# Zero products of TensorE in the pauses of a single-core, two-block network kernel

## What is computed

```python
def first_block(x, ...):                      # two layers
    # layer 0: recurrent block (projections, conv, gates, scan), layer 1: attention
    for layer in range(2):
        mix = rg_lru_block(x, ...) if layer == 0 else stick_breaking_attention(...) @ attn_w_out
        x = layer_norm(DN_ALPHA * x + mix, ln_g[layer, 0], ln_b[layer, 0])
        f = conv_ffn(x, ...)                  # 1024 -> 2 x 3072 -> 1024
        x = layer_norm(DN_ALPHA * x + f, ln_g[layer, 1], ln_b[layer, 1])

def second_block(x, c, ctx, ...):             # two layers, with 256 context tokens beside x
    for layer in range(2):
        h = rmsnorm(x, g) * (1 + sc1) + sh1   # shifts and gains from silu(c) @ mod_w
        x = x + g1 * mixer(h)                 # layer 0: Fourier and convolution; layer 1: softmax attentions
        h2 = rmsnorm(x, g) * (1 + sc2) + sh2
        x = x + g2 * hier_moe(h2)             # 32 experts of 1024 -> 512 -> 1024, 2 per token
    return rmsnorm(x, final_norm_g)
```

## Time and profile before

| | us |
|---|---|
| median of 3 runs | 2388.82 |
| lowest and highest | 2386.5, 2391.74 |
| the profiled execution | 2387.36 |
| its span, first to last instruction | 2385.3 |
| PE busy | 2134.5 (89%) |
| PE weight loads busy | 1330.0 (56%) |
| DVE busy | 849.8 (36%) |
| ACT busy | 368.4 (15%) |
| mean granted clock of PE | 0.953 |

### The profile page before, as it was taken

One profiled execution on the slowest core, in us unless ns is written; L12 is line 12 of the kernel. 1 busy time (PEld: TensorE's weight loads), 2 busy tenths in 40 slices (PEclk: granted clock), 3 DMA queues, 4 the chain that ended last, 5 costly groups with the idle time before them and its releaser, 6 DMA issues. The chain is left out here.

```text
span 2385.3 us, 27394 instructions
## 1 busy us (share of the span) xinstructions
PE 2134.5 (89%) x10410; PEld 1330.0 (56%) x10410; DVE 849.8 (36%) x1774; ACT 368.4 (15%) x695; POOL 23.6 (1%) x26
## 2 busy tenths in 40 slices
PE   7999998979999979979999999967989898888884
PEld 6788887657888844545444444425546433333332
DVE  3466664044666659441111111113263311111112
ACT  2411112042111130220000000002222100000001
POOL 0000000000000000000000000010000000000000
PEclk9999999999999989989999999988989899999997
DMA  7546556412566671306999999975221499999994
GB/s 272 212 177 247 211 211 246 162 50 90 213 247 241 215 298 42 135 36 278 427 428 426 427 426 426 426 311 213 74 103 71 186 426 427 427 428 427 426 427 186
DMA packets 138469, 638.09 MB, mean 268 GB/s; under 512 B 7120, under 2 KB 10224, under 8 KB 104496
## 3 DMA queue, kind: packets, MB, share of 16 engines
q1 hardware_dynamic: 120928, 595.48, 62.5%
q0 software_dynamic: 5600, 21.27, 2.5%
q10 hardware_dynamic: 11888, 20.62, 2.3%
HBM read 606.41 MB, written 30.93 MB: 267 GB/s over the span
## 5 line engine op out<-in xcount | busy, mean ns | idle before, releaser
L688 PE MATMUL T<-ring,S 128*64 128x512 f32 x2112 | 502.7, 632 | 71.7 <-DMA ring<-in_exp_w_up 68.5
L688 PEld LDWEIGHTS T<-ring,S 128*64 128x64 f32 x2112 | 157.3, 144 | 370.7 <-issue 365.0
L576 PE MATMUL T<-X,ring 128*128 128x256 f32 x1536 | 339.3, 380 | 2.4 <-ACT X L1036 2.4
L576 PEld LDWEIGHTS T<-X,ring 128*128 128x128 f32 x1536 | 292.1, 191 | 42.2 <-issue 2.6
L711 PE MATMUL T<-ring,S 128*64 128x512 f32 x1056 | 238.0, 592 | 1.2 <-DVE S L1529 1.2
L1325 DVE SCALAR_TENSOR_TENSOR S<-ring,cs,S 128x512 f32<-128x512 f32 x336 | 229.4, 744 | 0.0
L1523 DVE TENSOR_TENSOR S<-S,T 128x256 f32<-128x256 f32 x66 | 27.8, 421 | 498.0 <-ACT S L1104 498.0
L676 PE MATMUL T<-S 128*128 128x128 f32 x1600 | 188.2, 279 | 14.2 <-DVE S L1404 14.2
L676 PEld LDWEIGHTS T<-S 128*128 128x128 f32 x1600 | 185.2, 195 | 14.4 <-issue 7.9
L584 PE MATMUL T<-S,ring 128*128 128x256 f32 x768 | 176.7, 383 | 16.1 <-DVE S L1355 16.1
L584 PEld LDWEIGHTS T<-S,ring 128*128 128x128 f32 x768 | 143.4, 190 | 51.7 <-DVE S L1355 33.4
(11 more groups left out here) (265 smaller groups left out, 1452.0 us busy)
## 6 DMA issues: line engine op xcount, KB each, us to landing
ring<-in_exp_w_gate SPq DMA_DIRECT2D x66, 2048.0 KB, 16.6
ring<-in_exp_w_up SPq DMA_DIRECT2D x66, 2048.0 KB, 21.1
ring<-in_exp_w_down SPq DMA_DIRECT2D x66, 2048.0 KB, 23.4
ring<-in_ffn_w_up SPq DMA_DIRECT2D x24, 2048.0 KB, 12.7
ring<-in_mod_w SPq DMA_DIRECT2D x24, 2048.0 KB, 7.9
ring<-in_ffn_w_down SPq DMA_DIRECT2D x12, 2048.0 KB, 7.8
y_rows<-S ACTq DMA_DIRECT2D x132, 128.0 KB, 7.6
y_rows<-zb POOLq DMA_DIRECT2D x4, 3072.0 KB, 23.5
```

The lines of the kernel that those rows point to most:

```text
L576: ins = pe.matmul(T[:, m % 2, h * S:(h + 1) * S], w[:, k, m * P:(m + 1) * P], x1[:, k, :], start=(k == 0), stop=(k == KT - 1))
L688: ins = pe.matmul(T[c * B:(c + 1) * B, s, :].rearrange("p (g n) -> p g n", g=2), xgT[:, k, s * B:(s + 1) * B], ring[:, 3 * s:3 * s + 2, k ...
```

## The change

A helper `keep_busy(n, bank_)` issues n products of the zero tile with itself, 128 x 512 in bfloat16, into bank 5 or bank 1. They carry no semaphore and wait for none. Eleven calls are added.

```diff
+            def keep_busy(n, bank_=5):
+
+                for _ in range(n):
+                    pe.matmul(T[:, bank_, :], zb[:, 0:P], zb[:, :], start=True, stop=True)
+
             def layer_norm(i):
...
                 ins.then_inc(ln_mean, 1)
+                keep_busy(5)
...
                     if i == 0:
                         ins.then_inc(g_used, 2)
+                else:
+                    keep_busy(6)
                 pe.wait_ge(ln_rs, i + 1)
                 spread(S, LN_STD).then_inc(ln_bc, 1)
+                keep_busy(4, 1)
...
             def norm(r, k_tiles=KT, n=N2, sq=S1, off=0):
                 norm_sums(r, k_tiles, n, sq, off)
+                keep_busy(6)
                 norm_spread(r, n)
+                keep_busy(6)
...
                         ins.then_inc(full[u % 4], 1)
+                keep_busy(8)
                 pe.wait_ge(r["m_ready"], l + 1)
...
+                keep_busy(24 - 8 * l)
                 turn_tokens(t0)
                 up(t0, 0)
...
                 down(tl, 1)
+                keep_busy(80 - 20 * l, 1)
...
                 dense(c0["q"] + j, 4, lambda k: x1[:, k, :], u0["q"] + 2 * j, S)
+            keep_busy(12)
             read(pe, u0["q"] + 3)
             read(pe, u0["v"] + 3)
...
             pe.wait_ge(s_late, 16 * N_LATE)
+            keep_busy(20)
             norm(0)
...
                           start=True, stop=True).then_inc(full[(u + j) % 4], 1)
+            keep_busy(28)
             pe.wait_ge(cd_rot, 2)
```

## The result

| | before | changed |
|---|---|---|
| median, us | 2389.4 | 2371.27 |
| runs, lowest to highest, us | 6, 2386.15 to 2391.74 | 6, 2366.71 to 2376.81 |
| profiled execution, us | 2387.36 | 2370.43 |
| its span, us | 2385.3 | 2368.6 |
| mean granted clock of PE | 0.953 | 0.978 |

The ratio is 0.9928, with a 95% interval of 0.9916 to 0.994: 0.7% faster, 18.1 us. The forecast was 2370.3.

The account below looks back on a forecast made before the run. Outside the transfer-bound expert loops, PE spent 159.8 us at half clock, worth 39.3 us at most. The terms summed to -18.5 us: 2387.4 - 18.5 + 1.5 = 2370.3 us as a median, range 2362 to 2384.

Parts of the forecast that it names:

- the likeliest case: Whole kernel: the forecast itself, 18.5 us saved, median 2370.3 us, chance 0.68.
- Layer norms 0, 1, 3, norms 0, 2, 4: Work behind these norms returns to full clock: -1.6, -2.4, -4.2 (layer norm 3 with norm 0), -2.6, -2.1 us.
- Attention: 12 products ahead of the first scores, where only 0.69 us pause, delay ScalarE's read of them: +1.8 us.
- I count no clock gain: Attention: the long 3.52 us pause behind the scores stays empty, so no clock gain, at best 0.7 us.
- Layer norm 2: Has no low stretch in the earlier profile, so its products gain 0.
- Norm 3: 6.36 us of work at half clock, 3.2 at most; its sums keep empty gaps: -2.0 us.
- Route 0: 24 products leave 2.5 us empty and the clock may fall again; two thirds of 2.8 at most: -2.0 us.
- Route 1: Half of 6.29 us of work is 3.1; 16 products leave 2.9 us idle: -2.0 us.
- Last layer's attentions: 28 products fill 6.2 of 8.19 us; gain 2.5 at most, half taken because 2.0 us stay idle: -1.3 us.
- products at half clock and too many: Rival: zero products cost 0.44 us each and overrun the pauses, 49 us slower, 2437 us; chance 0.06.
- half of it given back: Rival: remaining idle and light work let the clock fall again; only 6 us gained, 2382.8 us; chance 0.18.
- the transposes: Rival: transposes hold the clock down for the 8 products behind them in each route; +1.4, 2371.7 us; chance 0.02.

Follow-up runs that it names:

- e1: The changed kernel with every zero product cut from 512 to 8 columns; 2391.69 us, ratio 1.0004 to the kernel before.
- e2: The changed kernel with zero products only in the layer norms, the norms and the 20 in front of norm 0; 2372.47 us, ratio 0.9932.
- e4: The changed kernel with the attention's 12 products removed and 14 put behind the first two heads' scores, in the pause before the suffix sums; 2367.07 us.
- e5: e4 with more products in the routes, behind the expert phases and before the last attentions, and 2 for 6 behind norms 2 and 4's spreads; 2366.76 us.
- e11: e4 without norm 3's 12 products and the 80 behind expert phase 0; 2368.79 us, ratio 0.992 to the kernel before.
- e3: The changed kernel with zero products only in the routes, before the attentions and before and behind the expert phases, none in layer norms and norms; 2387.94 us.
- e8: The changed kernel without the six and six zero products in norm 3; 2371.0 us, ratio 0.9918 to the kernel before.
- e6: The changed kernel without the 80 and 60 products behind the expert phases; 2372.54 us, ratio 0.9921 to the kernel before.
- e9: The changed kernel unchanged, profiled in a second execution; 2368.38 us.
- e7: The changed kernel with 24 instead of 12 products in front of the attention's first scores; 2370.77 us, ratio 0.9918 to the kernel before.

## Why the prediction was right, and where not

The changed kernel came out at 2371.27 for 2370.3: the likeliest case held, and it is right for its stated reason, by e1 (the clock) and e2 (the norms). That it is right to 1 us is partly luck: single terms were off by 2, with both signs, and the runs lie over 10 us.

Two readings in it were loose, and nothing hangs on them. A 9 in the earlier trace rows is 0.9 or more, so that row cannot tell 1.0 from 0.9. And the rank products' 5.6 us are not among PE's longest waits: its list of waits has, among others outside the loops, 16.1 us in the FFNs (18 waits), 13.0 in front of the suffix sums, 9.7 in front of the norms' sums and 8.2 in front of the last layer's scores. Of the terms:

- **Layer norms 0, 1, 3, norms 0, 2, 4.** Forecast 1.6 + 2.4 + 4.2 + 2.6 + 2.1 = 12.9, measured 1.55 + 2.33 + 4.26 + 2.62 + 1.90 = 12.66. The spreads are at 1.10 us. What worked was to take half of PE's work at half clock from the earlier trace rows, where the products behind have their operands. The prediction had only bounds for a zero product at half clock. The Trainium skill ("TensorE: Matmul & The Clock Gate", "Wait — 56ns, not 53.3ns?") has 427 ns for such a product at the low clock; the trace agrees. In the low stretch from 1617.2 three products stand between 1617.62 and the spread at 1618.90, 0.43 us each; six at full clock take 1.46 in all, 0.22 apart. Timeline of the changed kernel, norm 3:

```profile
1617.62 1.49 PE L544 MATMUL T<-zb 128*128 128x512 bf16 x3
1618.90 1.86 PE L537 MATMUL T<-std,tab 128*128 128x128 f32 x8
1620.60 1.46 PE L544 MATMUL T<-zb 128*128 128x512 bf16 x6
```

- **Attention: the step that was mis-sized, +1.8, measured +4.03.** The placement cost 1.55, as ScalarE's timeline shows: 3.46 us from its last read of the q products to the scores' in the changed kernel, 1.91 in e4 (two fences, in this order).

```profile
480.79 0.60 ACT L1093 ACTIVATE S<-T 128x512 f32<-128x512 f32 x1 [6.31 <-PE T L521]
...
484.25 0.60 ACT L1093 ACTIVATE S<-T 128x512 f32<-128x512 f32 x1 [1.55 <-PE T L820]
```

```profile
480.15 0.60 ACT L1094 ACTIVATE S<-T 128x512 f32<-128x512 f32 x1 [6.31 <-PE T L521]
...
482.06 0.60 ACT L1094 ACTIVATE S<-T 128x512 f32<-128x512 f32 x1
```

  That is near the 1.8 forecast. The other 2.5 us are the clock, and the step "I count no clock gain" left out that it could also be lost. The clock fell already in front of the first suffix sums, which before made at full clock (1.05 us more over the heads), and again at 528.3 in the output projection, 29.33 us where before took 27.89 in its first execution (1.44). The projection's part isn't the change's doing: e2, which has nothing in the attention, took 29.58 there, before's own second execution lost 1.6, and of 13 profiles eight lost 1.4 to 1.7 there. So the baseline of one execution was a lucky one here. The heads' part may be: the clock was low at the first suffix sums in all six profiles with products in front of the scores, in one of four with none or with 8 columns, and in none of three with 14 in the pause. Of e4's gain over the changed kernel, 1.55 us is shown to be placement. That 14 in the pause are better than none isn't shown: over the heads they gained 1.20, 1.20 and 0.10 us (e4, e5, e11) against before's first execution, and e2 without any gained 0.17.
- **Layer norm 2: 0, measured 0.19 with the FFN behind it, but only against before's first execution.** "Layer norm 2 has no low stretch" was true of one profile. In the three others without its full-width products (before again, e1, e3) the clock fell there, at a price of 1.7 to 3.6 us; in the nine with them it never did. This term was put at nothing from a single profile, and it is worth more than that.
- **Norm 3: -2.0, measured 0.** The step "6.36 us of work, 3.2 at most" counted work whose pace ScalarE's 16 passes set. e8 and e11 show that nothing hangs on these products. The same cover was allowed for in norm 4, and missed here.
- **Route 0: -2.0, measured -1.1 or -2.5.** "I take two thirds" is a mean over cases. If the clock falls in the gathering, 1.1 (also e6, e8, e11); if it falls in the zero products, 2.5 (e9), 2.7 (e7); in e4, where it was low ahead of them too, 1.5.
- **Route 1: -2.0, measured -2.95,** and once in eight profiles, in e6, -0.1. Again one of two cases. The gain is 2.9 when the clock holds through the pause of 2.9 us.
- **Last layer's attentions: -1.3, measured -1.84.** Half was too careful, though the clock fell at 1750.3.
- **Behind the expert phases: 0.** e6 and e11 bear it out at combine 0; at combine 1 the place gives 0.30 and 0.34 without the 60 (e2, e6) and 0.34 to 0.99 with them: 0.3 or so, unsure. Norm 5 with combine 1 gave 0.99 in all for 0.1.
- **Loops: 0.** 426 GB/s before and after, 0.16 and -0.54. They differ by 3 us and more between executions, with loop bodies that are all the same (loop 0: 3.08 gained in e8's, 1.77 in e4's, 0.53 lost in e1's; loop 1: 0.7 gained to 2.9 lost), and the first 106 us by 1.9. With the draws of the clock that could make up the 10 us over which the runs of the changed kernel lie; no run shows the sum.

The forecast sum was -18.5, the profiled execution gives -16.9. The errors are +2.2 (attention), +2.0 (norm 3), +0.9 (route 0) on one side, and 0.95 (route 1), 0.5 (last attentions), 0.9 (end) and 1.3 (ahead of everything, chance) on the other: they cancelled in part. Of the rivals, "products at half clock and too many" fell with 0.22 us at full clock; "half of it given back" is seen in the first profile only in route 0, and in e6 in route 1; the transposes didn't hold the clock down. The products behind route 1's transposes start 0.22 us apart ((1.67 - 0.38) / 6), in a window of full clock:

```profile
1839.62 1.67 PE L544 MATMUL T<-zb 128*128 128x512 bf16 x7
```

The Trainium skill ("TensorE: Matmul & The Clock Gate", "Part 4: PE-mode transpose") says that the full clock doesn't engage for transposes. By that they would be 0.44 apart; the trace doesn't agree, here as in the earlier trace rows.

## What to carry to other kernels

Lay windows over every low-clock stretch and price only the work in it whose operands are already there: here a dense product behind a norm paid half of its time, one that waited for ScalarE's passes paid nothing, and a transfer-bound loop paid nothing. Fill the pause itself with full-width products, a little less than the pause holds, and put them behind the products that another engine reads: in front of those, each one that stood out cost its 0.22 us. Where pauses of 2.9 to 3.5 us stayed, the clock fell in some executions and held in others. So profile both kernels twice before explaining 1 to 3 us of difference at such a place, and before pricing a place at nothing because one profile has no low stretch there.

## What the runs showed of the hardware

- The clock can fall or hold in the same order with the same pause: 2.91 us idle and 6.71 for the gathering in e6, 2.92 and 3.84 in the changed kernel; 3.52 us idle in front of the suffix sums at full clock in e2, and half clock behind 3.43 in the changed kernel.
- Layer norm 2's four zero products didn't always hold it: in the place behind them it was low from 574.1 in before's second execution, and in e1 and e3, but not in before's first. With 5 more behind the mean and 4 behind the spread it held in all nine profiles.
- Products of zeros in bfloat16, whose result nobody reads, keep the clock up for the float32 work behind them; the same products with 8 columns don't.
- Zero products are also a place where a fall costs nothing: 24 of them took 6.84 us for 5.34 in a pause that had room, and the real products behind ran at full clock.
